# First attention's keep sums from rounded high and low parts, and the first two weight panels in halves

## What is computed

```
h = rms_norm(x, norm_mix);  proj = h @ w_in            # q, k, v, pool and recurrence inputs, gates
# stick-breaking attention, 8 heads of 128, query blocks of 128:
z = q k^T * scale
log_beta = log_sigmoid(z)
log_keep = where(kpos < qpos, log_sigmoid(-z), 0)
after = cumsum(log_keep, reverse=True) - log_keep      # sum over the later keys
w = where(kpos < qpos, exp(log_beta + after), 0);  out = w @ v
```

## Time and profile before

| | us |
|---|---|
| median of 3 runs (lowest, highest) | 2564.46 (2559.68, 2565.71) |
| profiled execution | 2565.91 |
| its span, first to last instruction | 2564.1 |
| PE busy in the span | 2482.4 (97%) |
| DVE busy | 1310.1 (51%) |
| POOL busy | 1059.6 (41%) |
| ACT busy | 868.5 (34%) |
| mean granted clock of PE | 0.986 |

### The profile page before, as it was taken

The page is one execution under the profiler, slowest core; times in us unless marked ns, Lnnn a source line. Parts: engine busy times, 40 slices in busy tenths (PEclk is TensorE's granted clock), DMA queues, the critical chain, the costliest instruction groups (busy, mean ns, idle before and its releaser), DMA issues.

```text
span 2564.1 us, 30219 instructions
## 1 busy us (share of the span) xinstructions
PE 2482.4 (97%) x11742; PEld 1982.0 (77%) x11742; DVE 1310.1 (51%) x1960; ACT 868.5 (34%) x1360; POOL 1059.6 (41%) x830
## 2 busy tenths in 40 slices
PE   7999999999999999999989999999999889999998
PEld 6887767888888888876667778888888656788886
DVE  6336687543533321584756655596127855533301
ACT  4453345322322222334444433222224443322221
POOL 4322244544544444453222235454454222544442
PEclk9999999999999999999999999999999989999999
DMA  4212122322322233221111123232231012222232
GB/s 147 66 58 72 56 72 89 99 96 93 103 99 95 94 99 98 92 74 58 58 42 50 50 72 106 99 99 94 93 105 54 28 34 63 98 94 95 96 98 78
DMA packets 62574, 209.45 MB, mean 82 GB/s; under 512 B 6880, under 2 KB 9184, under 8 KB 62304
## 3 DMA queue, kind: packets, MB, share of 16 engines
q1 hardware_dynamic: 61424, 204.11, 24.3%
q10 hardware_dynamic: 1008, 3.41, 0.4%
HBM read 205.39 MB, written 2.10 MB: 81 GB/s over the span
## 4 chain that ended last, share of the span: by engine, by line
PE 86%; DVE 10%; ACT 2%; issue 1%; DMA 0%; DVEq 0%; ACTq 0%; SPq 0%
PE ps L617 24%; PE ps L619 24%; PE ps L618 24%; DVE T L2157 1%; PE ps L638 1%; PE ps L639 1%; PE ps L640 1%; PE ps L956 1%; PE ps L733 1%; ACT A L1594 1%; PE ps L725 1%; PE ps L970 1%; PE ps L984 1%; PE ps L754 1%; PE ps L756 1%
## 5 line engine op out<-in xcount | busy, mean ns | idle before, releaser
L588 POOL TENSOR_TENSOR w_lo<-w_raw,w_hi 128x512 fp32r<-128x512 f32 (+4 forms) x822 | 1049.9, 1301 | 1465.8 <-ACT w_hi L1290 1465.8
L617 PE MATMUL ps<-H,w_hi 128*128 128x512 f32 x1880 | 750.6, 399 | 22.6 <-DVEq L1852 12.9
L619 PE MATMUL ps<-H,w_lo 128*128 128x512 f32 x1880 | 736.5, 392 | 0.0
L618 PE MATMUL ps<-H,w_hi 128*128 128x512 f32 x1880 | 736.0, 391 | 0.0
L1290 ACT CAST w_hi<-w_raw 128x1024 fp32r<-128x1024 f32 (+4 forms) x411 | 403.0, 984 | 526.1 <-DMA w_raw<-in_weights_dram 519.7
L617 PEld LDWEIGHTS ps<-H,w_hi 128*128 128x128 f32 x1880 | 355.7, 189 | 110.4 <-issue 21.3
L617 PE MATMUL ps<-split,w_hi 128*128 128x512 f32 x1034 | 410.4, 397 | 6.9 <-issue 3.7
L619 PEld LDWEIGHTS ps<-H,w_lo 128*128 128x128 f32 x1880 | 355.2, 189 | 75.3
L618 PEld LDWEIGHTS ps<-H,w_hi 128*128 128x128 f32 x1880 | 355.9, 189 | 71.2 <-issue 1.7
L619 PE MATMUL ps<-split,w_lo 128*128 128x512 f32 x1034 | 404.2, 391 | 0.0
L618 PE MATMUL ps<-split,w_hi 128*128 128x512 f32 x1034 | 403.7, 390 | 0.0
(11 more groups left out here) (408 smaller groups left out, 2423.2 us busy)
## 6 DMA issues: line engine op xcount, KB each, us to landing
w_raw<-in_weights_dram SPq DMA_DIRECT2D x323, 512.0 KB, 3.6
w_raw<-in_weights_dram SPq DMA_DIRECT2D x48, 448.0 KB, 3.2
w_raw<-in_weights_dram SPq DMA_DIRECT2D x22, 256.0 KB, 2.6
X<-in_xt_dram SPq DMA_DIRECT2D x4, 512.0 KB, 7.9
out_dram<-A SPq DMA_DIRECT2D x8, 256.0 KB, 2.1
w_raw<-in_weights_dram SPq DMA_DIRECT2D x12, 128.0 KB, 2.0
w_raw<-in_weights_dram SPq DMA_DIRECT2D x6, 192.0 KB, 2.3
A<-in_w_gates_dram ACTq DMA_DIRECT2D x1, 1024.0 KB, 4.8
```

What stands on the lines that cost most here:

```text
L588: sub = nc.gpsimd.tensor_tensor(w_lo[:, p % NS, c], w_raw[:, p % NS, c], w_hi[:, p % NS, c].bitcast(F32), ALU.subtract)
L617: mm_(ps[:, bank, :], r(wh), xh, start=(k == 0), stop=False)
L618: mm_(ps[:, bank, :], r(wh), xl, start=False, stop=False)
L619: mm = mm_(ps[:, bank, :], r(wl), xh, start=False, stop=(k == kt - 1))
```

## The change

1. The softplus values of a step now stay in T. They are then copied to a rounded high part and the rest is stored as a low part (two new DVE instructions in `keep`, with waits on earlier sums, since the high and low parts take the room that two copies of SP had; the last block of odd heads goes to the room of ACC). The mask product L1973 is now waited for.
2. The sums L754 and L756 take the rounded mask "after" and a column "one" spread over 128, each times the high and then the low part.
3. x is loaded in five parts (two single k tiles first), panels 0 and 1 in halves with semaphores of their own; casts, low parts and PE's first pair go by halves, PE starting with two units of tile 0, two of tile 1, then by turns. Only the first 8 columns of the vectors are loaded first; the rest comes later, on one semaphore with constants and masks. The gate weights share a semaphore with the late constants.

```diff
-    ("ident", 128), ("ones", 128), ("after", 128), ("causal01", 128), ...
+    ("ident", 128), ("ones", 128), ("causal01", 128), ...
-MASKS = [..., ("pick", 16), ("head", 4)]
+MASKS = [..., ("pick", 16), ("head", 4), ("after", 128), ("one", 1)]
+        at_acc = nc.sbuf_base
         ACC = sb("ACC", [P, S])[:]
+        last_parts = nc.alloc_sbuf_tensor_at("last_parts", [P, 2 * P], F32R, offset=at_acc)
-        SP = area(12288, 2, 1280)
+        SP_HI, SP_LO = rounded(12288, 1280), rounded(12288 + 1280, 1280)
+
+        def keep_parts(n, j):
+
+            if j == 3 and n % 2:
+                return last_parts[:, 0:P], last_parts[:, P:2 * P]
+            at = slice(TRIK[j], TRIK[j] + S - P * j)
+            return SP_HI[:, at], SP_LO[:, at]
+        X_PART = (0, 1, 2, 2, 3, 3, 4, 4)
...
+            def half_panel(p, half):
+                src = weights[PSTART[p]:PSTART[p] + P * PSIZE[p]].rearrange("(p c) -> p c", p=P)
+                c = slice(HALF * half, HALF * half + HALF)
+                sp.dma_start(w_raw[:, p, c], src[:, c]).then_inc(w_loaded[p] if half else s_w0[p], 16)
-            panel(0)
             x_part(0)
-            panel(1)
+            half_panel(0, 0)
             x_part(1)
+            half_panel(1, 0)
+            half_panel(0, 1)
             x_part(2)
+            half_panel(1, 1)
             x_part(3)
+            x_part(4)
...
+            def low_half(p, half):
+                c = slice(HALF * half, HALF * half + HALF)
+                if half:
+                    pool.wait_ge(w_hi_ready[p], 1)
+                else:
+                    pool.wait_ge(s_hi0, p + 1)
+                sub = nc.gpsimd.tensor_tensor(w_lo[:, p, c], w_raw[:, p, c], w_hi[:, p, c].bitcast(F32), ALU.subtract)
+                sub.then_inc(w_ready[p] if half else s_lo0, 1)
+            for half in range(2):
+                low_half(0, half)
+                low_half(1, half)
...
-            together("qk_a", (0, 1), HX, (s_h, H_BASE["mix"]))
-            pe.wait_ge(s_con, 16)
+            first = [units(("qk_a", t), HX, (s_h, H_BASE["mix"])) for t in range(2)]
+            run(first[0], 2)
+            run(first[1], 2)
+            for _ in zip(*first):
+                pass
+            run(first[1], 8)
+            pe.wait_ge(s_con, 48)
...
-                    mm_(bank[:, 0:w], con("after"), SP[:, n % 2, TRIK[j]:TRIK[j] + w], start=True, stop=False)
+                    hi, lo = keep_parts(n, j)
+                    mm_(bank[:, 0:w], mask("after"), hi, start=True, stop=False)
+                    mm_(bank[:, 0:w], mask("after"), lo, start=False, stop=False)
                     for jj in range(j + 1, 4):
-                        mm_(bank[:, P * (jj - j):w], con("ones"), SP[:, n % 2, TRIK[jj]:TRIK[jj] + S - P * jj],
-                            start=False, stop=False)
+                        for part in keep_parts(n, jj):
+                            mm_(bank[:, P * (jj - j):w], mask("one").to_broadcast([P, P]), part, start=False, stop=False)
...
-            act.dma_start(V_[:], vectors).then_inc(s_vec, 16)
-            hi_to(2)
+            act.dma_start(V_[:, 0:8], vectors[:, 0:8]).then_inc(s_scale, 16)
+            high_half(0, 0)
+            high_half(1, 0)
+            high_half(0, 1)
+            act.dma_start(V_[:, 8:NV], vectors[:, 8:NV]).then_inc(s_con, 16)
             act.dma_start(C_[:], consts).then_inc(s_con, 16)
-            act.dma_start(MASKS32, masks).then_inc(s_msk, 16)
+            act.dma_start(MASKS32, masks).then_inc(s_con, 16)
+            high_half(1, 1)
...
-                sp_ = SP[:, n % 2, TRIK[j]:TRIK[j] + w]
+                sp_ = T[:, c % 2, 0:w]
+                hi, lo = keep_parts(n, j)
                 dve.wait_ge(s_l, c + 1)
-                if j == 3 and n >= 2:
-                    dve.wait_ge(s_aft, 4 * n - 4)
-                link(v.scalar_tensor_tensor(sp_, z, 0.0, T[:, c % 2, 0:w], ALU.max, ALU.add))
+                link(v.scalar_tensor_tensor(sp_, z, 0.0, sp_, ALU.max, ALU.add))
...
-                v.tensor_tensor(sp_[:, 0:P], sp_[:, 0:P], con("causal01"), ALU.mult).then_inc(s_sp, 1)
+                link(v.tensor_tensor(sp_[:, 0:P], sp_[:, 0:P], con("causal01"), ALU.mult))
+                if j == 3 and n >= 2:
+                    dve.wait_ge(s_aft, 4 * n - 4)
+                if j == 2 and n >= 1:
+                    dve.wait_ge(s_aft, 4 * n)
+                link(v.tensor_copy(hi, sp_))
+                v.tensor_tensor(lo, sp_, hi.bitcast(F32), ALU.subtract).then_inc(s_sp, 1)
```

More of the change, by code:

```diff
@@ L31 @@
 SLOT = 1024
+HALF = 512
 STAGE = {
@@ L141 @@
 CONSTS = [
-    ("ident", 128), ("ones", 128), ("after", 128), ("causal01", 128), ("rot64", 128), ("rot32", 128),
+    ("ident", 128), ("ones", 128), ("causal01", 128), ("rot64", 128), ("rot32", 128),
     ("pool_inv", 64), ("eps", 1), ("freq64", 1), ("freq32", 1),
@@ L150 @@
 NC_ = _at
-MASKS = [("ident", 128), ("big_keep", 128), ("neg_future", 128), ("neg_chunk", 128), ("pick", 16), ("head", 4)]
+MASKS = [("ident", 128), ("big_keep", 128), ("neg_future", 128), ("neg_chunk", 128), ("pick", 16), ("head", 4), ("after", 128), ("one", 1)]
 MCOL = {}
@@ L177, in constants @@
     c["after"] = (i[:, None] > i[None, :]) * 1.0
+    c["one"] = np.ones((P, 1))
     c["causal01"] = (i[:, None] < i[None, :]) * 1.0
@@ L322, in rounded @@
             assert at + n <= ARENA
-            if at not in split_tiles:
-                split_tiles[at] = nc.alloc_sbuf_tensor_at(f"split{at}", [P, n], F32R, offset=at_a + 4 * at)
-            return split_tiles[at][:]
+            if (at, n) not in split_tiles:
+                split_tiles[at, n] = nc.alloc_sbuf_tensor_at(f"split{at}_{n}", [P, n], F32R, offset=at_a + 4 * at)
+            return split_tiles[at, n][:]
         def parts_at(hi, lo, step_hi=S, step_lo=S):
@@ L458, in build @@
         s5 = small[:, 64:256].rearrange("p (a b) -> p a b", a=12)
-        s_xin = [sem(f"x_loaded{i}") for i in range(4)]
-        s_vec, s_con, s_msk, s_late, s_gw, s_pos = (sem("vectors_loaded"), sem("consts_loaded"), sem("masks_loaded"), sem("late_loaded"),
-                                             sem("gate_w_loaded"), sem("positions_loaded"))
+        s_xin = [sem(f"x_loaded{i}") for i in range(5)]
+        X_PART = (0, 1, 2, 2, 3, 3, 4, 4)
+        s_scale = sem("first_scales_loaded")
+        s_w0 = [sem(f"first_half_loaded{p}") for p in range(2)]
+        s_hi0, s_lo0 = sem("first_halves_rounded"), sem("first_halves_ready")
+        s_con, s_late, s_pos = (sem("vectors_consts_masks_loaded"), sem("gate_w_then_late_loaded"), sem("positions_loaded"))
         w_loaded = [sem(f"w_loaded{i}") for i in range(NS)]
@@ L610, in units @@
                 for p, k0, n in PARTS[tile]:
-                    pe.wait_ge(w_ready[p % NS], p // NS + 1)
+                    if p < 2:
+                        pe.wait_ge(s_lo0, p + 1)
+                    else:
+                        pe.wait_ge(w_ready[p % NS], p // NS + 1)
                     for k in range(k0, k0 + n):
+                        if p < 2 and P * k == HALF:
+                            pe.wait_ge(w_ready[p], 1)
                         if arrive:
@@ L1926, in _ @@
             rms("mix")
-            dve.wait_ge(s_msk, 16)
+            dve.wait_ge(s_con, 48)
             link(v.tensor_copy(CR[:], MASKS32))
             dve.sem_inc(s_cr, 1)
-            dve.wait_ge(s_con, 16)
+            dve.wait_ge(s_con, 48)
             copy_rms("mix")
```

38 lines of the change are left out of this document (24 added, 14 removed).

## The result

| | before | changed |
|---|---|---|
| median of 7 runs each (lowest, highest) | 2563.89 us (2559.68, 2565.71) | 2574.51 us (2567.35, 2577.15) |
| ratio of the two, 95% interval | | 1.0040 (1.0030 to 1.0049) |
| profiled execution, its span | 2565.91, 2564.1 | 2567.35, 2565.5 |

The change makes the kernel slower by 10 us. I had forecast no change (2564) and a range that ended at 2574; the time lies just above it, on the side of the rival "DVE pays in full". The profiled execution of the changed kernel is the fastest of its seven, so its trace shows only part of the loss: at the end of the attention it is 9.1 us behind the kernel before, and at the end of its span 1.4, because behind the attention the granted clock happened to be low for less time.

What follows compares the result with a forecast made beforehand. PE follows DVE in the start, PE bounds half A, both are nearly full in half B. Start -3.8, half A -5.2 and half B +8.9 gave -0.1 us, so 2564 us, range 2553 to 2574.

Steps and rivals of the forecast that it cites:

- DVE pays in full: Rival, half B: GpSimd disturbs each keep, 23 us added on DVE, 17 lost; 2572 to some 2578 us; chance 0.20.
- The start: Before the attention: DVE's first scaling at 4.3 instead of 7.21, its end at 22.9 instead of 26.7; 3.8 us saved.
- Half A: First half of the first attention, PE the bound: PE's 7.6 us arrive less stall and gaps, 5.2 us saved.
- the stall at the head scaling: Half A, PE's 2.45 us stall at 197.21: keep ahead 1.5 us longer, and 0.6 us of PE's gain lost.
- PE's saving: Sums L754 and L756 as rounded products: 1.9 us a head saved, 7.6 a half, 15.1 in all.
- Half B: Second half of the first attention, PE and DVE nearly full: 8.9 us lost, bounds -7.6 to +17.
- The price: DVE's added copies and subtractions in half B: 17 us with waits, 13 undisturbed, 23 if GpSimd hits 12 of 32.
- The share absorbed: Half B up to 293.7: 11.5 us added on DVE, waits absorb 2.3 and some 3.6, eviction L2035 5.6 later.
- DVE busy some 128: Sign in half B: DVE busy some 128 us, with a PE stall of 5 us or more before the second pool_mix.
- The clock: Half B: the long PE stall before the second pool_mix brings the low clock level, about 1.4 us more.
- DVE's slack takes it: Rival, half B: DVE's 43 us unused time covers the added 17, PE's saving arrives; 2545 us; chance 0.24.
- Short products are dear: Rival: rounded products at 256 and 128 columns take f32's time; half A some 5 us longer, 2574; chance 0.02.

Runs made afterwards that it cites:

- e1: Changed kernel with the attention's sums and keeps as before in both halves, so only the new start remains: 2561.28 us, 0.9994 of the kernel before.
- e2: Changed kernel with half B's sums and keeps as before, so new start and rounded parts in half A only: 2556.27 us, 0.9975 of the kernel before.
- e9: Changed kernel with both added DVE operations of half B moved behind evictions and pooling: 2559.79 us, 0.9979 of the kernel before.
- e4: Changed kernel, but in half B DVE writes the softplus rounded, without low part, and PE multiplies the high part twice: 2552.88 us, 0.9960 of before.
- e3: Changed kernel, but in half B DVE makes both parts and PE sums only the high parts in plain f32: 2571.18 us, 1.0036 of before.
- e10: Changed kernel with half B's sums and keeps as before, but DVE's subtraction from z there made twice: 2561.82 us, 0.9988 of the kernel before.
- e13: Changed kernel with half B's sums and keeps as before, but DVE's subtraction from z there made three times: 2562.66 us, 1.0003 of the kernel before.

## Why the prediction was wrong

**The start: the sum right, its parts partly by luck.** The sum had 3.8; the profile shows 3.7 at the first logits, and e1's clock-neutral mean 2.9. DVE's last pair ended 4.9 us earlier, not 3.8, and then a stall that I had not seen took 1.2 back. "What follows in this stage moves as a whole" was wrong there. On the way DVE waited 1.6 us for an x part that I had taken as present, and GpSimd's second stretch began at 16.6, not at 15.0.

**Half A: right in kind, a little small.** Forecast 5.2, measured 4.7 clock-neutral (e1 to e2). The one forecast obstacle, the stall at the head scaling, grew as said. PE's saving was 1.6 instead of 1.9 a head: each of the four steps saved 0.06 to 0.1 less than forecast, whatever its width. The profiled execution shows only 2.6 less, because the clock fell for longer behind the grown stall: 1.7 of it.

**Half B: the step that failed is what DVE's addition costs there.** Two of its terms were wrong.

*The price.* I priced the 32 operations at 17 us with their waits, by the means of the same operations of the splitting (L1843, L1844), and put the disturbed case at 23 as the upper bound, with 12 of 32 hit. They took 27.25, with 14 hit and 1.0 us more for each. In half B those operations of the splitting stand behind the evictions and the ladder. The new ones stand ahead of both, and took on themselves what had fallen on the ladder (7 us less there) and more. My count of hits by GpSimd's share of busy time came near (12 for 14), but I kept it for the bound alone. The Trainium skill's rule (SBUF — State Buffer, "Who interferes with whom") pointed to the upper figure: an operation with two SBUF inputs, or a copy in a two-port mode, fully blocks against a GpSimd operation that reads SBUF. The trace agrees: the 128-column subtraction of the changed kernel takes 1.29 us at one place and 0.29 at another where GpSimd is idle, the 512-column copy 1.38 against 0.43 in e9.

*The share absorbed.* Up to the second `pool_mix` I had 11.5 us added, 5.9 absorbed by DVE's waits and 5.6 late. The eleven keeps' new operations took 16.7 there; DVE as a whole was busy 9.7 more (68.5 to 78.2), as the ladder gave back; and PE was 7.7 late at equal clock. So DVE's waits absorbed 1.9 and not 5.9. The one at the exponent did shrink by 2.3 as said, from 3.36 to 1.09; the others together gave nothing. That half of the added time seems absorbed, as forecast, is luck: 7 of the 9 us are time that older operations, the ladder above all, no longer took. For the same reason "DVE busy some 128" came true with a wrong price. I also saw three growing stalls where there are eleven.

Without the clock I had 7.5 us for half B. The cuts of the two profiles show 10.2, and the means 12.0 (e2 to changed). PE's saving in B is worth 3.2 us alone (e4) and about 2 beside DVE's operations (e3's 2534.0 against 2531.9, with an error of 0.9).

**The clock: missed.** I put one fall of 1.4 us. In half B it is 5.1 more than before, in both profiles; over twelve runs the whole kernel loses 5.9 more than before and 6.4 more than e2. Six stalls of half B have 2.4 us or more, for two before; the earlier trace rows held the hint, that a 2.63 us stall was followed by the low level. Behind the six stalls there are four falls, one of them long, where I had drawn one more than before.

By rivals: "DVE pays in full" had the mechanism (keeps disturbed by GpSimd, 23 us or more added) and the time (2572 to 2578), and I gave it 0.20. "DVE's slack takes it" is refuted by e3. "Short products are dear" is refuted by e4, which is faster than e2.

**What stays open.** How much of e9's gain is the smaller amount on DVE and how much the order. Why the clock falls behind some stalls of 2.5 to 3 us and not behind others, and how much of the 6 us stands outside half B: there the falls differ between two executions with equal stalls, and e3, with nearly the same stalls in B, lost only 35.7 (error 1.8). And why e10's first 8 us cost 0.79 a microsecond and e13's 16 only 0.53. The repeats were undisturbed, but the mask product behind them was not: 7.7 us in the kernel before, 10.6 in e10 and 12.5 in e13. Counted with that, the added time ahead of the evictions costs 0.58 and 0.40.

## To carry to other kernels

Before adding work to an engine that feeds the bound one, list what its queue delivers behind the new instructions, and put them behind that: e9 changes two lines' place and wins 0.5% back. Price an SBUF operation on DVE by rows at the place where it will stand, not by the mean of its kind, and where GpSimd's subtractions run there, price it at the blocked duration. Then ask which older operations get their time back; the sum over the engine can look right while the work ahead of the evictions is far too cheap in the forecast. Take a change of PE's work per stage: the same products gave 4.7 us where PE was the bound and about 2 where DVE was, and the best version has them in half A alone.

## What the hardware showed that I had not expected

- Two profiled executions of one kernel had all their stalls of half B equal within 0.06 us and differed by 5.9 us in what the granted clock took (34.3 and 40.2), so the profile of one execution can be 7 us off its kernel's median (2567.35 against 2574.51) with no difference in its attention.
- A blocked DVE operation of the 14 pays about 1 us whatever its own size: 128 columns 0.29 to 1.31 us, 384 columns 0.36 to 1.37, 512 columns 0.43 to 1.38. It ends shortly after the GpSimd subtraction that it met.
- The clash moves with the work. 7 us of it left the ladder when new operations stood ahead of it, and in e9 5 came back. Its total isn't kept: beyond the 13.1 us of the undisturbed operations, DVE was busy 5.6 us more in the changed kernel and no more in e9.
